# Two transformer blocks on one core: VectorE's split of a weight part in the forgetting attention, moved behind the norm and the copy

## What is computed

```python
# q, k, v: 16 heads of 64, 16 meta rows and 512 rows; c is the running sum of log f
for each query block of 128 rows, for each head:
    s = (q @ k.T) / 8 + (c_q - c_k)             # over the meta rows and the rows up to here
    s = where(key position <= query position, s, -inf)
    p = softmax(s)
    o = p @ v
y_att = o * silu(z_att)
# z_att, q, k, v and the gates come from u @ w_in
```

## Time and profile before

| what | value |
|---|---|
| median of 3 runs | 2473.33 us (2471.67 to 2474.66) |
| the profiled execution, its own time | 2474.97 us |
| its span, first to last instruction | 2472.9 us |
| mean granted TensorE clock | 0.994 of full speed |
| busy: PE, DVE, ACT, POOL | 2402.8, 1297.1, 880.1, 375.3 us |
| the steps of the forgetting attention | from 2012 to about 2316 us |

### The profile page before, as it was taken

The page is one execution under the profiler, slowest core; times in us unless marked ns, Lnnn a source line. Parts: engine busy times, 40 slices in busy tenths (PEclk is TensorE's granted clock), DMA queues, the critical chain, the costliest instruction groups (busy, mean ns, idle before and its releaser), DMA issues.

```text
span 2472.9 us, 34710 instructions
## 1 busy us (share of the span) xinstructions
PE 2402.8 (97%) x14354; PEld 2008.6 (81%) x14354; DVE 1297.1 (52%) x2101; ACT 880.1 (36%) x1499; POOL 375.3 (15%) x301
## 2 busy tenths in 40 slices
PE   7999999999999999999999999999999999999999
PEld 6678888888887777656888887988989878877788
DVE  3775625543535776785333336366565445554433
ACT  4332111211224544434222224364545333444422
POOL 0210000000014444501000001143343410000000
PEclk9999999999999999999999999999999999999999
DMA  9734334334321111112333332221222121121222
GB/s 325 202 101 120 120 110 129 120 120 119 107 64 35 52 51 35 35 51 69 97 91 102 98 90 86 69 69 52 69 69 80 58 69 52 52 69 52 80 91 111
DMA packets 252744, 220.79 MB, mean 89 GB/s; under 512 B 7480, under 2 KB 243443, under 8 KB 252204
## 3 DMA queue, kind: packets, MB, share of 16 engines
q1 hardware_dynamic: 249072, 217.92, 29.0%
q10 hardware_dynamic: 3260, 0.58, 0.1%
q0 software_dynamic: 256, 0.07, 0.0%
HBM read 214.26 MB, written 6.29 MB: 89 GB/s over the span
## 4 chain that ended last, share of the span: by engine, by line
PE 59%; ACT 3%; DVE 3%; issue 2%; POOL 1%; DVEq 0%; ACTq 0%; POOLq 0%
PE two L688 10%; PE bank L1357 5%; PE bank L1548 4%; PE bank L688 4%; PE bank L1353 3%; PE bank L1334 3%; PE two L1288 3%; PE bank L1529 2%; PE bank L1054 2%; PE two L1159 2%; PE bank L1185 2%; PE two L1568 2%; PE bank L1024 1%; PE bank L1036 1%; PE two L1300 1%
## 5 line engine op out<-in xcount | busy, mean ns | idle before, releaser
L2573 DVE TENSOR_TENSOR wL<-ring,wH 128x512 fp32r<-128x512 f32 x224 | 181.9, 827 | 225.2 <-ACT wH L1843 225.0
L1834 ACT ACTIVATE wH<-ring 128x2048 fp32r<-128x2048 f32 (+1 forms) x80 | 149.2, 1864 | 270.9 <-PE bank L693 72.9
L2562 DVE TENSOR_TENSOR wL<-ring,wH 128x2048 fp32r<-128x2048 f32 (+1 forms) x80 | 178.9, 2236 | 81.2 <-ACT wH L1834 80.9
L688 PE MATMUL two<-h1H,wH 128*128 128x512 f32 x496 | 195.2, 394 | 0.0
L688 PE MATMUL two<-h1H,wL 128*128 128x512 f32 x496 | 193.4, 390 | 0.0
L688 PE MATMUL two<-h1L,wH 128*128 128x512 f32 x496 | 193.2, 390 | 0.0
L1843 ACT ACTIVATE wH<-ring 128x512 fp32r<-128x512 f32 x224 | 133.6, 623 | 58.5 <-PE bank L1334 21.0
L1913 ACT ACTIVATE gateS<-two 128x512 f32<-128x512 f32 x44 | 26.3, 598 | 330.0 <-PE bank L693 141.8
L2666 DVE SCALAR_TENSOR_TENSOR xT<-two,ada,xT 128x512 f32<-128x512 f32 (+1 forms) x48 | 30.6, 680 | 184.9 <-PE bank L693 65.7
L1357 PE MATMUL bank<-unH,wH 128*128 128x272 f32 (+1 forms) x368 | 112.0, 304 | 3.8 <-ACT cin L2104 2.1
L688 PEld LDWEIGHTS two<-h1H,wH 128*128 128x128 f32 x496 | 93.1, 188 | 20.5 <-issue 1.2
(11 more groups left out here) (646 smaller groups left out, 6963.2 us busy)
## 6 DMA issues: line engine op xcount, KB each, us to landing
ring<-in_ffn_w_in SPq DMA_DIRECT2D x88, 512.0 KB, 5.1
ring<-in_w_in SPq DMA_DIRECT2D x40, 1024.0 KB, 5.2
ring<-in_w_ada SPq DMA_DIRECT2D x32, 1024.0 KB, 5.2
ring<-in_ffn_w_out SPq DMA_DIRECT2D x16, 1024.0 KB, 5.2
early<-in_w_ada SPq DMA_DIRECT2D x12, 1024.0 KB, 12.0
ring<-in_diff_w_in SPq DMA_DIRECT2D x12, 1024.0 KB, 5.2
ring<-in_w_proj_ssd SPq DMA_DIRECT2D x8, 1024.0 KB, 5.0
ring<-in_ffn_w_out SPq DMA_DIRECT2D x8, 768.0 KB, 4.6
```

The costliest lines, as they stand in the source:

```text
L688: m = nc.tensor.matmul(bank[3 * s + half], w, r[:, 0:LAT], start=i == 0, stop=i == n - 1)
L1834: nc.scalar.activation(hi, raw, ACT.Copy).then_inc(w_hi, 1)
L2562: nc.vector.tensor_tensor(lo, raw, hi.bitcast(F32), ALU.subtract).then_inc(w_lo, 1)
L2573: nc.vector.tensor_tensor(lo, raw, hi.bitcast(F32), ALU.subtract).then_inc(q_lo, 1)
```

## The change

In VectorE's loop over the 64 steps the call of `split_lo_part` moves behind `fox_norm(u + 1)` and `fox_kept(u)`. Nothing is added or removed; the programs of the other engines and the DMA queues are the same.

```diff
@@ -3135,10 +3135,10 @@
                     fox_max(u + 1)
                 if u % 8 == 1 and u > 8:
                     fox_gate(u // 8 - 1)
-                split_lo_part(S_OF[UNITS[m]] + 1, r)
                 if u < 63:
                     fox_norm(u + 1)
                 fox_kept(u)
+                split_lo_part(S_OF[UNITS[m]] + 1, r)
                 if u % 8 == 1 and u > 8:
                     fox_lo(u // 8 - 1)
             second_dve(("gs", 2))
```

## The result

The changed kernel takes 2460.27 us, the median of 6 runs (2456.50 to 2460.69); the kernel before, on the same chip, 2473.32 us (6 runs, 2471.67 to 2475.61). The ratio is 0.9945 with a 95% interval of [0.9934, 0.9956]: faster, by 13.05 us between the medians. The profiled execution took 2460.63 us.

What follows compares the result with a forecast made beforehand. TensorE, busy 2402.8 of 2472.9 us, was taken as the bound. Shorter waits for the copy (7.97 us) plus two clock falls gone (3.17) made 11.14 us, so 2463.0 us, range 2460.5 to 2467.2.

Steps and rivals of the forecast that it cites:

- What bounds the kernel, and the chain: TensorE bounds it, busy 2402.8 of 2472.9 us; VectorE's split needlessly stands ahead of norm and copy, which the scores await.
- the eight places named: Scores of steps 6, 22, 38, 54, 23, 39, 55 and 62, where TensorE waits 8.70 us in all for VectorE's copy.
- 1.13 us earlier at steps 6, 22, 38, 54 and 1.14 at step 62: Norm and copy come that much earlier; the waits give back 4.52 us at the four steps and 1.14 at step 62.
- Steps 23, 39, 55: Scores waiting 0.77 us each for the copy; all of it goes, 2.31 us in total.
- At step 7 and at step 63 there is no such stall before: TensorE was slow there; the spare time is about nought to 0.4 us, counted as nothing.
- The clock, 3.17 us: Falls to half clock behind the stalls of steps 6 and 62, 1.58 and 1.59 us; both go, bounds 0 and 3.17.
- the rule of the Trainium skill: Ties clock falls to idle gaps longer than any here; rival: falls stay, gain 7.97 us, 2467.0 or 2465.4, chance 0.25.
- The median: Median of the three runs before, 1.64 us below the profiled execution; the summed gain taken from it gives 2462.2 us.
- I take the middle: Forecast of 2463.0 us, between 2463.8 from the profiled execution and 2462.2 from the median.
- the low end of 2460.5: Range's lower bound: 2462.2 us less 1.7 us for the spread of the runs.
- The margins: Spare time of delayed work: split 2.67 us, copy against the turn 1.85 and 0.61 us, next maximum not late; cost nothing.

Runs made afterwards that it cites:

- experiments 1 to 3: Against the kernel before, VectorE's order: 1 norm, split, copy, 2467.40 us; 2 copy, norm, split, 2459.07 us; 3 the change in nine of 64 steps alone, 2463.18 us.
- eight traces with hardly a wait: Changed kernel three times, copy first twice, change in nine steps alone, each split twice, split of the step before; copy waits 1.3 us or less each.
- the kernel with nine waits: The change in all but nine of the 64 loop steps, against the kernel before: median 2470.91 us, ratio 0.9998, stage 292.11 us.
- experiment 7: Kernel before with the new order in loop steps 4 and 60 alone: one execution, 2469.14 us, stage 291.49 us.
- experiment 10: Order of the kernel before, but VectorE splits the part of the step before: median 2461.56 us, ratio 0.9949 against the kernel before.

## Why the prediction was right, and where it was wrong

- *What bounds the kernel, and the chain.* Right. The change acts by the copy's time (experiments 1 to 3), nearly all of it in the eight places named and at the two steps behind the falls, and nothing takes the gain back behind the stage: from the scores of step 63 to the end it is 165.4 us in both traces.
- *1.13 us earlier at steps 6, 22, 38, 54 and 1.14 at step 62.* Right to 0.02 us, with the wait that stays at step 62 (0.49 forecast, 0.51 found).
- *"Steps 23, 39, 55: ... all of it goes ... 3 x 0.77 = 2.31 us."* This is the first half of the step that failed, the price of a wait. The term was mis-sized: these places gave 2.99. A wait's price is not the idle time shown.
- *"At step 7 and at step 63 there is no such stall before ... I count nothing."* Those two are in the term of the clock. But the sum counts nothing for waits that show no idle time, and that is the second half: steps 15, 31 and 47 gave 0.78 us in all. I could have found them by the 0.42 us from copy to scores.
- *The clock, 3.17 us.* The size was right for the trace in hand (3.16), but in part by luck. The rows of the chain gave 2040.91 and 2307.64 for the scores of steps 7 and 63; in the timeline they start at 2040.75 (below) and 2307.48. So 6.12 us should have been 5.97. And the 4.54 us without a fall is too long by the same 0.16, since it takes away 0.77 for a wait of 0.93. Both falls went, yet 3.17 was the wrong price for the median. In an execution without falls the stage of the kernel before lasts some 293.8 us, so the change is worth 11.4 us there, and each fall adds 0.6. By the rule of the Trainium skill that I set against the rows ("TensorE: Matmul & The Clock Gate", section "HAM oscillation — how this bites in real kernels") the falls had another cause than these waits and could have stayed. These traces do not agree with it: all seven falls of the stage sit at waits of 1.19 to 2.93 us, and none of eight traces with hardly a wait has one. Yet the kernel with nine waits has none either. Waits go with falls here, but what decides whether one falls stays open.
- *The median, "I take the middle", and the low end of 2460.5.* The low end was the median before less the sum, less the spread of the runs before. The sum was too small by 1.46 us, nearly all of it by the two halves above (0.68 and 0.78), and that put the result outside: with the 12.60 us of the stage the same working gives 2460.7 from the median, and 2459.0 for the low end. Taking the middle made the forecast's gain smaller still, on the ground that a fall is worth 1.6 us, where it is worth 0.6. The other part of the miss is luck. The spread of the runs before was taken for that of the runs to come, and the runs spread by falls outside the stage: in the fourteen traces the stage begins anywhere from 2010.1 to 2015.0 us, with one and the same program up to there. Side by side with the kernel before, the changed kernel gained 13.05, 9.54 and 11.24 us between the medians, and its other two medians, 2463.04 and 2462.54, lie inside the range. The stage itself gives 11.4 to 12.6.
- *The margins.* Those of the split and of the maximum held. What is thin is the cover behind the copy, which I gave no number for: one more split fits nearly everywhere, two do not.

The row of the timeline for the scores of step 7 in the kernel before:

```profile
2040.75 1.15 PE L1568 MATMUL two<-kA,qA 66*128 66x512 f32 x4
```

## What to carry to other kernels

On an in-order engine, ask of each instruction in a chain which of its operands comes last. Work whose operand is made after the chain's own (here the split, whose high part ScalarE makes after the exponential) goes behind the chain, or is done one step later, which gave the same gain here; and an instruction that needs none of the late results (here the copy) goes ahead of them. Price a wait of TensorE by the distances from start to start of its neighbours, not by the idle time in brackets, and look for hidden waits by the fixed distance from releaser to waiter. When gains are under 1%, compare the stretch that the change touches, since falls of the clock elsewhere move the whole time by more.

## What was not expected of the hardware

A fall of the granted clock to 0.50 behind a wait cost 0.62 us where the distance to the next scores grew by 1.58 against a full clock without a wait, because the slow TensorE came too late to wait for the next copy. And the same program reaches the same instruction, the scores of step 0, up to 4.9 us apart in different executions. Falls of the clock before it go with that: in the trace that is there first (2010.09 us, experiment 7) the clock stands at 0.50 in four stretches before that point, in the one that is there last (2014.99, experiment 10) in eight. That these falls are all of the difference is not shown.
